# Loading expert weights in pairs: one 2 MB transfer for two neighbouring 1 MB units

## The reference, cut to what matters

```python
E, D_FF_EXPERT = 8, 3584            # experts, hidden width of one
y = jnp.zeros_like(xt)              # xt: (256, 1024)
for e in range(N_EXPERTS):
    y = y + gates[:, e:e + 1] * swiglu(xt, w_gate[e], w_up[e], w_down[e])
# swiglu(x, wg, wu, wd) = (silu(x @ wg) * (x @ wu)) @ wd
```

## Time and profile before

| what | value |
|---|---|
| time, median of 3 runs | 1365.17 us (1362.48 to 1369.05) |
| span of the profiled execution, first to last instruction | 1365.5 us |
| mean granted clock of TensorE | 0.992 |
| PE, DVE, ACT busy, share of the span | 98%, 81%, 71% |
| moved by DMA | 433.24 MB, mean 317 GB/s |
| expert weights | 336 transfers of 1024 KB |
| median from issue to landing: gate, up, down units | 9.9, 9.3, 9.7 us |

### The profile page before, as it was taken

How to read it: one execution, slowest core, us unless ns; L and a number is a source line. 1 busy time by engine, 2 the same in 40 slices (tenths; PEclk the granted TensorE clock), 3 DMA queues, 4 the chain that set the end, 5 groups by cost and what they waited for, 6 DMA issues and landing times.

```text
span 1365.5 us, 18288 instructions
## 1 busy us (share of the span) xinstructions
PE 1331.8 (98%) x7233; PEld 1123.6 (82%) x7233; DVE 1107.3 (81%) x885; ACT 975.5 (71%) x930; POOL 168.7 (12%) x103
## 2 busy tenths in 40 slices
PE   8989999999999999999999999999999999999996
PEld 7888999999999778777877888777877877787784
DVE  4664655555666599999999989999999999999995
ACT  5465544446556667888788878888888888878883
POOL 4251000000000132574400000000000000000001
PEclk8999999999999999999999999999999999999998
DMA  9305755554542389999999999999999999999992
GB/s 372 121 1 185 207 186 184 184 184 154 204 144 86 111 332 401 404 419 407 412 421 419 421 401 390 422 421 421 408 411 421 414 411 421 421 411 422 418 418 98
DMA packets 67203, 433.24 MB, mean 317 GB/s; under 512 B 8160, under 2 KB 10336, under 8 KB 18992
## 3 DMA queue, kind: packets, MB, share of 16 engines
q1 hardware_dynamic: 60320, 418.01, 76.4%
q0 software_dynamic: 3360, 12.22, 3.0%
q10 hardware_dynamic: 3440, 1.91, 0.8%
HBM read 426.09 MB, written 6.03 MB: 316 GB/s over the span
## 4 chain that ended last, share of the span: by engine, by line
PE 74%; DVE 11%; DMA 9%; ACT 4%; issue 1%; SPq 0%; DVEq 0%; ACTq 0%
PE banks L1887 21%; PE banks L1889 20%; PE banks L1888 20%; DMA raw<-in_moe_w_gate 9%; DVE w_lo L1169 6%; ACT w_hi L623 2%; PE banks L2451 2%; DVE qk_lo L1169 2%; PE banks L2120 2%; PE banks L2452 2%; ACT qk_hi L623 1%; PE banks L2108 1%; PE banks L2488 1%; PE banks L2490 1%; PE banks L2462 1%
## 5 line engine op out<-in xcount | busy, mean ns | idle before, releaser
L1169 DVE TENSOR_TENSOR w_lo<-raw,w_hi 128x2048 fp32r<-128x2048 f32 (+1 forms) x312 | 711.2, 2297 | 134.4 <-ACT w_hi L623 132.9
L623 ACT CAST w_hi<-raw 128x2048 fp32r<-128x2048 f32 (+1 forms) x312 | 592.5, 1909 | 161.8 <-PE banks L1889 125.5
L1169 DVE TENSOR_TENSOR qk_lo<-raw,qk_hi 128x2048 fp32r<-128x2048 f32 x84 | 192.0, 2286 | 13.0 <-ACT qk_hi L623 12.1
L623 ACT CAST qk_hi<-raw 128x2048 fp32r<-128x2048 f32 x84 | 160.0, 1905 | 14.3 <-PE banks L1889 9.5
L1887 PE MATMUL banks<-w_hi,t_hi 128*128 128x512 f32 (+2 forms) x444 | 164.7, 371 | 2.9 <-DVE w_lo L1169 1.5
L1889 PE MATMUL banks<-w_lo,t_hi 128*128 128x512 f32 (+2 forms) x444 | 161.6, 364 | 0.0
L1888 PE MATMUL banks<-w_hi,t_lo 128*128 128x512 f32 (+2 forms) x444 | 161.5, 364 | 0.0
L1887 PE MATMUL banks<-t_hi,w_hi 128*128 128x256 f32 x544 | 155.5, 286 | 0.9 <-DVE t_lo L1190 0.9
L1888 PE MATMUL banks<-t_hi,w_lo 128*128 128x256 f32 x544 | 154.3, 284 | 0.0
L1889 PE MATMUL banks<-t_lo,w_hi 128*128 128x256 f32 x544 | 154.2, 284 | 0.0
L1887 PE MATMUL banks<-w_hi,h_hi 128*128 128x512 f32 x300 | 118.8, 396 | 0.2 <-DVE w_lo L1169 0.2
(11 more groups left out here) (358 smaller groups left out, 2261.9 us busy)
## 6 DMA issues: line engine op xcount, KB each, us to landing
raw<-in_moe_w_gate SPq DMA_DIRECT2D x112, 1024.0 KB, 9.9
raw<-in_moe_w_up SPq DMA_DIRECT2D x112, 1024.0 KB, 9.3
raw<-in_moe_w_down SPq DMA_DIRECT2D x112, 1024.0 KB, 9.7
raw<-in_na_w_qkv SPq DMA_DIRECT2D x12, 1024.0 KB, 4.8
raw<-in_ffn_w_gate SPq DMA_DIRECT2D x11, 1024.0 KB, 5.0
raw<-in_ffn_w_up SPq DMA_DIRECT2D x11, 1024.0 KB, 5.1
raw<-in_ffn_w_down SPq DMA_DIRECT2D x11, 1024.0 KB, 4.9
raw<-in_w_in_e SPq DMA_DIRECT2D x6, 1024.0 KB, 15.7
```

Source lines behind the costliest of these rows:

```text
L623: act.copy(tile_hi(u, n), raw[:, u.raw, 0:n]).then_inc(hi_done, 1)
L1169: dve.tensor_tensor(tile_lo(u, n), raw[:, u.raw, 0:n], tile_hi(u, n).bitcast(F32), ALU.subtract).then_inc(lo_done, 1)
```

## The change

The two units of gate, of up and of down of one step are laid side by side in DRAM, so that each partition's 16 KB are contiguous, and one DMA of 2 MB loads both into two neighbouring raw buffers. The six buffers then work as three pairs, each pair with a semaphore of its own. `hi` of either unit waits for the whole pair. `lo`, the high and low buffers, the matmuls and their order are as before. A pair may be issued when VectorE has finished with both units of the pair that lay there, so from `load_pair(i)` the wait is for unit i - 5, where the first of the two units waited for i - 6 before. The place in the ring is moved by one buffer (`(paired + 2) % RING`), so that a pair never wraps. The first pairs wait for the buffers' earlier users, units of the attention's output projection.

```diff
+PAIRS = RING // 2
...
     @property
     def raw(self):
-        return self.s % RING
+        return self.s % RING if self.paired is None else (self.paired + 2) % RING
+
+    @property
+    def pair(self):
+        return self.paired // 2 % PAIRS
...
     def filled(self):
-        return self.k * 16 + 16 * (self.s // RING + 1)
+        if self.paired is not None:
+            return 16 * (self.paired // RING + 1)
+        in_pairs = E * MOE_UNITS if self.s >= U_MOE else 0
+        return self.k * 16 + 16 * ((self.s - in_pairs) // RING + 1)
...
+        pair_full = [sem(f"pair_full{i}") for i in range(PAIRS)]
...
+            def load_pair(i, src):
+
+                sp.wait_ge(lo_done, U_MOE + i - 4 if i >= RING else min(U_MOE + i - 3, U_MOE))
+                u = moe_unit(i)
+                dst = raw[:, u.raw:u.raw + 2, :].rearrange("p r c -> p (r c)")
+                sp.dma_start(dst, src).then_inc(pair_full[u.pair], 16)
...
-            gate_up(0, 0, U_MOE, [(0, i, 0) for i in range(4)])
+            for i, w in enumerate((moe_w_gate, moe_w_up)):
+                load_pair(2 * i, w[0, 0])
...
-                    for i, w in enumerate((moe_w_gate, moe_w_gate, moe_w_up, moe_w_up)):
-                        load_block(moe_unit(6 * n - 2 + i), w[expert[v], j, i % 2])
+                    for i, w in enumerate((moe_w_gate, moe_w_up)):
+                        load_pair(6 * n - 2 + 2 * i, w[expert[v], j])
                 v, j = ORDER[n - 1]
-                for i in range(2):
-                    load_block(moe_unit(6 * n + (2 if n < STEPS else -2) + i), moe_w_down[expert[v], j, i])
+                load_pair(6 * n + (2 if n < STEPS else -2), moe_w_down[expert[v], j])
...
-                act.wait_ge(raw_full[u.raw], u.filled())
+                act.wait_ge(raw_full[u.raw] if u.paired is None else pair_full[u.pair], u.filled())
...
-        by_step = inputs[n].reshape(E, 2, 4, P, MOE_STEPS, HALF).transpose(0, 4, 1, 3, 2, 5)
-        arrays[f"in_{n}"] = np.ascontiguousarray(by_step).reshape(E, MOE_STEPS, 2, P, UNIT)
+        by_step = inputs[n].reshape(E, 2, 4, P, MOE_STEPS, HALF).transpose(0, 4, 3, 1, 2, 5)
+        arrays[f"in_{n}"] = np.ascontiguousarray(by_step).reshape(E, MOE_STEPS, P, 2 * UNIT)
```

More of the change, by code:

```diff
@@ L183, with __init__ @@
 class Unit:
-    def __init__(self, s, k=0, part=None, behind=PARTS):
-        self.s, self.k, self.own, self.behind = s, k, part, behind
+    def __init__(self, s, k=0, part=None, behind=PARTS, paired=None):
+        self.s, self.k, self.own, self.behind, self.paired = s, k, part, behind, paired
     def count(self, ahead=0):
@@ L501, in moe_unit @@
             return Unit(U_MOE + i, 0, (U_MOE + turn) % PARTS if turn < PARTS else PARTS,
-                        PARTS if i < PARTS else PARTS + 1)
+                        PARTS if i < PARTS else PARTS + 1, i)
         def unit_of(base, e, c, j=0):
@@ L558, in gate_up @@
                 for i, w in enumerate((moe_w_gate, moe_w_gate, moe_w_up, moe_w_up)):
-                    load_block(unit_of(base, *c[i]), w[e, j, i % 2])
+                    load_block(unit_of(base, *c[i]), w[e, j, :, i % 2 * UNIT:(i % 2 + 1) * UNIT])
             def down(e, j, base, c):
                 for i in range(2):
-                    load_block(unit_of(base, *c[i]), moe_w_down[e, j, i])
+                    load_block(unit_of(base, *c[i]), moe_w_down[e, j, :, i * UNIT:(i + 1) * UNIT])
             def middle(e, j, base, sweep):
@@ L601, in _ @@
             with sp.If(n_over > SLOTS):
+                sp.wait_ge(lo_done, U_MOE + E * MOE_UNITS)
                 for again in range(1, SWEEPS):
@@ L896, in _ @@
             split_group_hi(4, 1, (3, 6))
-            for i in range(3):
-                hi(Unit(U_OUT1 + 3 + i))
+            hi(Unit(U_OUT1 + 3))
+            for i in range(2):
+                hi(moe_unit(i))
             warm(ACT.Sqrt)
@@ L914, in _ @@
             warm(ACT.Silu)
-            hi(Unit(U_MOE + 2))
+            hi(moe_unit(2))
             def gather_hi(v, sweep):
@@ L1500, in _ @@
             split_group_lo(4, 1, (3, 6))
-            for i in range(3):
-                lo(Unit(U_OUT1 + 3 + i))
+            lo(Unit(U_OUT1 + 3))
+            for i in range(2):
+                lo(moe_unit(i))
             residual_by_half(3, OUT_BANK, U_OUT1 + 3)
@@ L2747 @@
     for n in ("moe_w_gate", "moe_w_up"):
-        by_step = inputs[n].reshape(E, 2, 4, P, MOE_STEPS, HALF).transpose(0, 4, 1, 3, 2, 5)
-        arrays[f"in_{n}"] = np.ascontiguousarray(by_step).reshape(E, MOE_STEPS, 2, P, UNIT)
-    by_step = inputs["moe_w_down"].reshape(E, MOE_STEPS, 2, 2, P, D).transpose(0, 1, 2, 4, 3, 5)
-    arrays["in_moe_w_down"] = np.ascontiguousarray(by_step).reshape(E, MOE_STEPS, 2, P, UNIT)
+        by_step = inputs[n].reshape(E, 2, 4, P, MOE_STEPS, HALF).transpose(0, 4, 3, 1, 2, 5)
+        arrays[f"in_{n}"] = np.ascontiguousarray(by_step).reshape(E, MOE_STEPS, P, 2 * UNIT)
+    by_step = inputs["moe_w_down"].reshape(E, MOE_STEPS, 2, 2, P, D).transpose(0, 1, 4, 2, 3, 5)
+    arrays["in_moe_w_down"] = np.ascontiguousarray(by_step).reshape(E, MOE_STEPS, P, 2 * UNIT)
     arrays["in_tables"] = constants()
```

## The result

The changed kernel takes 1464.28 us (median of 4 runs, 1460.7 to 1466.74), the kernel before 1365.10 us beside it. The ratio is 1.071, 95% interval 1.069 to 1.073: 99 us slower. The forecast was 1367 us, its range 1357 to 1386.

A forecast was written before the change was run, and what follows sets the result against it. Loads were taken to pace only after 1000 us, PE, ACT and DVE before; faster loads -2.2, lead +2.4 and disturbance +2 us gave +2.2 on the 1365.5 us span, 1367.7; median 0.3 lower, so 1367 us, range 1357 to 1386.

The forecast's parts named there:

- What bounds the kernel before: Expert stage: loads pace only from 1000 to 1316 us, where faster loads alone could give at most 4.1 us.
- The saving per pair: Weight queue: halving the packets saves 0.085 us per pair, so a step needs 14.66 us of it instead of 14.92.
- Landing to release, 7.3 us: Gate pair: from ACT's start on the first unit to DVE's end on the second, 7.3 us.
- Issue to landing, L = 7.3 us: Weight transfers: a 2 MB pair lands 7.3 us after its issue, bounds 7.2 to 9.6.
- rival 1: Ring of three paces alternating steps: 4.2 us per 0.1 us of L above 7.4; 1382 us at L = 7.7; chance 0.28.
- The ring becomes a bound as tight as the others, and this is what decides.: Ring of three pairs: a place comes round in 14.75 to 14.8 us, reserve 0.1 us where it was 5.7.
- Big steps that follow each other: 0: Successive big steps: about 16 us each, over a loop of 14.8, so no change.
- Both signs: Forecast wrong if a couple of steps changes by over 0.3 us, or successive big steps change at all.
- The lead, the disturbance: Expert stage: first units come 2.49 us later, +2.4 us once; POOL's transfers delay one landing, +2 us.
- the start and the end: First down pair lands before ACT wants it, 0; last pair costs 0 to +1.4 us, taken as 0.
- Rival 2: Loads pace more of the stage than the waits show: 1351 us, or 1358 for half of it; chance 0.16.
- rival 3: Packets stay at 8 KB, so the queue still needs 14.92 us a step: about 1371.5 us; chance 0.14.

The follow-up runs named there:

- e10: Changed kernel, but from the 7th pair on each transfer brings only the first unit (1 MB), the second keeping old data: 1362.78 us, ratio 0.997.
- e12: Kernel before, with two extra stretches as seventh and eighth single buffers from the 12th unit on: 1360.80 us, ratio 0.997.
- e4: Changed kernel, but each 2 MB transfer reads the old DRAM layout, so packets stay at 8 KB: 1461.7 us, ratio 1.071.
- e1: Changed kernel, but each pair comes by two 1 MB transfers issued one right after the other: 1453.87 us, ratio 1.067.
- e5: Kernel before, with five of the six buffers working in the expert steps: 1370.87 us, ratio 1.003.
- e6: Kernel before, with four of the six buffers working in the expert steps: 1466.52 us, ratio 1.071.
- e2: Changed kernel, but two 1 MB transfers per pair, each half with its own semaphore, so only the issue is late: 1368.86 us, ratio 1.002.
- e3: Changed kernel, but each 1 MB half is issued when its own buffer is free, so only the use is late: 1375.02 us, ratio 1.007.
- e7: Changed kernel, plus a fourth pair of buffers from the 13th pair on, filled by two 1 MB transfers: 1365.76 us, ratio 0.999.
- e9: Changed kernel, but from the 7th pair on VectorE computes only half the columns of each low part: 1405.47 us, ratio 1.030.
- e11: Changed kernel, plus a fourth pair of buffers from the 6th pair on, filled by two 1 MB transfers: 1368.19 us, ratio 1.002.
- e8: Kernel before, with two extra stretches as seventh and eighth single buffers from the 27th unit on: 1363.78 us, ratio 0.998.

## Why the prediction was wrong

The forecast took the right loop and put a wrong number into it: 7.3 us from issue to landing, where the stage has 10.0. Step by step:

- **What bounds the kernel before.** Right as far as the runs tell. Loads cost little: e10 and e12 gain 2.4 and 4.4 us, with intervals of about 2 to 6, against at most 4.1 us that I had read from the waits.
- **The saving per pair.** Right. 0.085 us per pair was forecast; pairs that follow without a gap land 4.88 us apart (1178.48 to 1183.36) where 2 x 2.487 = 4.97 were needed, and in e4, with 8 KB packets, pairs without a gap are 4.97 us apart too. It is worth nothing here, since the queue is not full. (By 435 GB/s the saving would be 0.07 us, not the 0.08 of the prediction. The 0.6 us per step in the expectation of e12 were too much as well: 3 x 0.09 us is what the landings show.)
- **Landing to release, 7.3 us.** Right: 7.1 in the rows above, 6.8 to 7.1 by kind of pair.
- **Issue to landing, L = 7.3 us. This term failed.** It was the 4.8 us of a transfer that finds the queue empty, plus a second MB at the stream's rate, with 7.2 to 9.6 as bounds. The measured 10.0 us lie above even the upper bound. With 0.15 + 10.0 + 6.95 the loop is 17.1 us, and the stage moves 6.29 MB at 369 to 374 GB/s, 16.8 to 17.05 us a step. The error has two parts. The small one, 0.7 us, is that a pair takes 8.0 us even alone; 0.5 of it are the 16 KB packets, since e4 has 7.5. By itself it makes a loop of 0.15 + 8.0 + 6.95 = 15.1 us, by the rule of rival 1 worth some 10 us. The large one, 2.0 us, is to have taken a transfer that finds the queue empty for one in a queue with other pairs in it. e1 shows it without the other: its two 1 MB transfers land 7.4 us after the first was issued in the one place where the trace has both landings of a gate pair that found the queue empty (446.38 to 453.76 us), near the forecast, and its gate pairs take 9.6 us (median) from 1030 to 1260 us, at 1453.87 us for the whole. e5 and e6 show it in the kernel before.
- **"The ring becomes a bound as tight as the others, and this is what decides."** It did decide, not as one of several but alone. "Now it has 0.1" was in truth 2.2 us less than nothing.
- **Big steps that follow each other: 0.** Wrong by the same term. At 14.8 us the loop would have hidden under their 16 us; at 17.05 it does not, and all 56 steps lose. Both signs that the prediction had set for being wrong came: the couple of steps takes 17.85 + 16.56 = 34.4 us instead of 29.65, and the big steps that follow each other changed.
- **The lead, the disturbance, the start and the end,** +2.4, +2, 0 and 0: too small to be seen in 99 us. e2 and e3, which have one half of the lateness each, lose 2.3 and 8.5 us in all; how that divides was not measured.
- **The rivals.** Rival 1 happened. Its rule, 4.2 us for each 0.1 us of L, gives with the loop at 17.05 us 24 x 2.2 + 18 x 2.1 = 91 us for the alternating steps and some 1 us for each of the 14 others, 105 us, where 99 were measured. That the sum comes so near is in part luck, for the 1 us of the big steps is a rough figure. But the rival was priced at L = 7.7 and given 0.28, and the range ended at L = 7.8, although the prediction's own bound was 9.6. Rival 2 and rival 3 did not happen; the packets became 16 KB.

The warning stood in the rows. The earlier trace rows showed 10.6 us from issue to landing and I called all over 4.8 "queueing", a reserve of 5.7 us. Only part of it was. No row of before showed a transfer that was issued late into a busy queue, and e6 is the measurement that was missing: 6.9 us.

The Trainium skill's fit for one DMA on GpSimd's path ("DMA: Bandwidth & Descriptors", Anatomy of one DMA), 2.0 us and bytes over 436 GB/s, gives 6.8 us for 2 MB. The transfers here are issued by SyncE. The trace has 8.0 alone and 10.0 in the stage, so for this purpose it would have misled further than my own sum.

What stays open is why a transfer that is issued late into a busy queue needs more than its turn. Of the 10.0 us a good part is the turn: the up pair above waits 5.1 us for the pair ahead of it and then takes 4.88, as one in a full stream does. The gate pair of 1185.74 waits 2.7 us and then takes 6.37, where 8.0 - 2.7 = 5.3 would do if it went as fast as one alone. The runs show this extra time, and not by what part of the path it comes.

## What to carry to other kernels

Before transfers are merged, write down the loop of one buffer: issue to landing as it is in the busy stage, plus landing to release, over the number of places, and compare it with the time that the stage has per place; merging two buffers takes reserve away at the issue and again at the use, and in this kernel each was nearly free (+0.2% and +0.7%) while both were not (+6.7%). The time of a transfer that finds the queue empty is not the term to put in; shorten the ring of the unchanged kernel by one and by two places and see where it breaks (here it bore one, +0.3%, and not two, +7.1%). Here one more place was worth the whole 99 us, and the larger packets, once the ring was long enough, nothing that shows.

## What was not expected of the hardware

- In this kernel a stream that keeps the queue full needs its next 2 MB issued about 5 us before the transfer ahead of it lands. Issued 5.1, 3.3 and 2.7 us ahead, pairs landed 4.88, 5.06 and 6.37 us after the one before (rows of the changed kernel above). Over the 117 pairs of the changed kernel from the 52nd on the median gap between landings was 4.88 us for those issued 5 to 6 us ahead (29 pairs), 5.31 for 4.3 to 5 (20), 5.71 for 3.5 to 4.3 (23) and 6.28 for 2.5 to 3.5 (30). A pair as fast as one alone, 8.0 us from its issue, would have had gaps of at most 5.5 us in the last group and 4.88 in the others. With 8 KB packets (e4) it is nearly the same: 4.97, 5.21, 5.52 and 6.17 us.
- Packets of 16 KB on SP's queue go with slower transfers of POOL beside them. The median from issue to landing of POOL's seven gathers was 9.4 us before and 12.0 in the changed kernel, with the queue less full; of e4, which has the same 2 MB transfers in 8 KB packets, it was 9.8. In the other runs it was 11.2 to 11.9 where most packets are of 16 KB (e7, e9, e11) and 9.5 to 10.8 where they are of 8 KB and all weights are loaded (e1, e2, e3, e5, e6, e8, e12). Lines of the pages' DMA part, first of before, then of the changed kernel and of e4:

```profile
arena<-x_rows,arena POOLq DMA_INDIRECT x7, 9.4
```

```profile
arena<-x_rows,arena POOLq DMA_INDIRECT x7, 12.0
```

```profile
arena<-x_rows,arena POOLq DMA_INDIRECT x7, 9.8
```
